# One group of products per attention step on TensorE, in place of two or three, in a two-layer transformer kernel

## The reference

```
# block 1: "dilated" attention, 8 heads of 64, three (window, dilation) patterns
s = q k^T + bias;  s = where(mask, s, NEG);  p = exp(s - max)
o = (p v) / sum(p)          # the three patterns joined by a softmax of their log-sums
# block 2: stick-breaking attention, 8 heads of 64, queries in blocks of 128
z = q k^T * scale;  sp = where(causal, softplus(z), 0)
rest = reverse_cumsum(sp) - sp
w = where(causal, exp(log_sigmoid(z) - rest), 0);  o = w v
```

## Time and profile before

| | us |
|---|---|
| three timed runs | 1364.08, 1364.75, 1364.88 |
| their median | 1364.75 |
| profiled execution, first to last instruction (span) | 1363.0 |
| TensorE busy in it | 1355.1 |
| VectorE, ScalarE, POOL busy | 872.2, 817.7, 335.4 |
| first attention on TensorE, from, to | 171.3, 231.5 |
| second attention on TensorE, from, to | 673.2, 793.4 |

### The profile page before, as it was taken

How to read it: one execution, slowest core, us unless ns; L and a number is a source line. 1 busy time by engine, 2 the same in 40 slices (tenths; PEclk the granted TensorE clock), 3 DMA queues, 4 the chain that set the end, 5 groups by cost and what they waited for, 6 DMA issues and landing times.

```text
span 1363.0 us, 19642 instructions
## 1 busy us (share of the span) xinstructions
PE 1355.1 (99%) x7510; PEld 1136.7 (83%) x7510; DVE 872.2 (64%) x1604; ACT 817.7 (60%) x1267; POOL 335.4 (25%) x306
## 2 busy tenths in 40 slices
PE   9999999999999999999999999999999999999999
PEld 6977966789899898887777878888888898889889
DVE  6055466577576672356498789975436785558557
ACT  6575666753544545666488677775656645754553
POOL 0211100235353251111211111211113262315214
DMA  7976643925436138876765575668888536824723
GB/s 250 241 170 137 148 117 86 224 32 195 99 101 175 34 124 192 192 169 143 154 138 122 132 198 124 134 145 184 196 212 206 113 137 174 185 47 160 191 52 109
DMA packets 57970, 202.46 MB, mean 149 GB/s; under 512 B 6450, under 2 KB 7019, under 8 KB 57748
## 3 DMA queue, kind: packets, MB, share of 16 engines
q0 software_dynamic: 25632, 93.09, 36.7%
q1 hardware_dynamic: 31380, 106.24, 23.6%
q10 hardware_dynamic: 864, 1.87, 0.4%
HBM read 199.05 MB, written 2.12 MB: 148 GB/s over the span
## 4 chain that ended last, share of the span: by engine, by line
PE 93%; ACT 2%; DMA 2%; DVE 1%; POOL 1%; issue 1%; SPq 0%; ACTq 0%; POOLq 0%; DVEq 0%
PE bank L644 23%; PE bank L651 23%; PE bank L648 23%; PE bank L682 15%; PE bank L840 2%; PE bank L816 2%; PE bank L830 1%; PE bank L797 1%; PE bank L865 1%; DMA WH<-in_w_in 1%; DMA RAW<-in_w_in 1%; PE bank L848 1%; POOL quarters_s L2182 0%; DMA quarters<-in_w_ff 0%; POOL quarters L2182 0%
## 5 line engine op out<-in xcount | busy, mean ns | idle before, releaser
L644 PE MATMUL bank<-NH,WH 128*128 128x512 f32 x1152 | 463.3, 403 | 0.4 <-ACT NH L1191 0.2
L648 PE MATMUL bank<-NL,WH 128*128 128x512 f32 x1152 | 448.2, 390 | 0.5 <-DVE NL L1453 0.5
L651 PE MATMUL bank<-NH,WL 128*128 128x512 f32 x1152 | 448.1, 390 | 0.4 <-DVE WL L1448 0.4
L644 PEld LDWEIGHTS bank<-NH,WH 128*128 128x128 f32 x1152 | 216.5, 188 | 62.1 <-issue 19.7
L651 PEld LDWEIGHTS bank<-NH,WL 128*128 128x128 f32 x1152 | 216.2, 188 | 46.7 <-DVE WL L1448 0.8
L648 PEld LDWEIGHTS bank<-NL,WH 128*128 128x128 f32 x1152 | 216.5, 188 | 45.4 <-issue 2.6
L1010 ACT ACTIVATE WH<-RAW 128x1024 fp32r<-128x1024 f32 (+3 forms) x148 | 151.9, 1031 | 76.4 <-PE bank L651 39.5
L682 PE MATMUL bank<-AH,WH 128*128 128x256 f32 x644 | 182.6, 284 | 0.5 <-DVE gains_hT L1830 0.3
L682 PE MATMUL bank<-AL,WH 128*128 128x256 f32 x644 | 182.2, 283 | 0.0
L682 PE MATMUL bank<-AH,WL 128*128 128x256 f32 x644 | 182.2, 283 | 0.0
L1018 ACT ACTIVATE WL<-WH 128x1024 fp32r<-128x1024 f32 (+1 forms) x146 | 153.2, 1051 | 21.4 <-DMA WH<-in_w_in 19.1
(11 more groups left out here) (371 smaller groups left out, 2130.5 us busy)
## 6 DMA issues: line engine op xcount, KB each, us to landing
WL<-in_w_in POOLq DMA_DIRECT2D x58, 512.0 KB, 6.3
RAW<-in_w_gu SPq DMA_DIRECT2D x44, 512.0 KB, 5.4
WL<-in_w_gu POOLq DMA_DIRECT2D x34, 512.0 KB, 7.8
RAW<-in_w_ff SPq DMA_DIRECT2D x32, 512.0 KB, 4.7
WH<-in_w_in POOLq DMA_DIRECT2D x32, 512.0 KB, 6.4
RAW<-in_w_in SPq DMA_DIRECT2D x28, 512.0 KB, 6.3
quarters<-in_w_ff SPq DMA_DIRECT2D x24, 512.0 KB, 4.7
WL<-in_w_ff POOLq DMA_DIRECT2D x17, 512.0 KB, 6.1
```

Source lines behind the costliest of these rows:

```text
L644: e.matmul(o, a[0], a[1], start=(k == 0), stop=False)
L648: e.matmul(o, b[0], b[1], start=False, stop=False)
L651: mm = e.matmul(o, c[0], c[1], start=False, stop=(k == t.kt - 1))
```

## The change

The generator `attention` gets a function `when(s)` in place of a start, a step and an offset. All three kinds of product of a step are due at one time, in the order transposes, scores, values. In the first attention that is the step's start (the scores move forward by 0.57 units); in the second it is 3.36 units after the start, where the scores stood, and 1.68, 0 and -3.36 in the last three steps, which have no scores. On ScalarE the exponential of the second attention now stands before the copies to wT, and on VectorE the copy out (`heads_out`) is due after the group. The mask or bias step of the first attention is due with the scores, 0.57 units earlier.

```diff
+        def dil_time(s):
+            return T_A1 + R1 * s
+
+        def stick_time(s):
+            return T_A2 + R2 * s + 1.68 * (2 if s < NA else (1, 0, -2)[s - NA])
...
-            def attention(name, T, R, q, apart, qs, ks, vs, zbuf, wbuf, q_key, k_key, v_keys, fence):
+            def attention(name, when, qs, ks, vs, zbuf, wbuf, q_key, k_key, v_keys, fence):
                 for s in range(NA + 3):
-                    yield T + R * s + 0.1
+                    yield when(s) + 0.1
                     if s == 0:
                         pe.wait_ge(*fence)
+                    if 2 <= s <= NA + 1:
+                        hp, i = ORDER[s - 2]
+                        for p in range(2):
...
+                                mm = e.transpose(bank[:, j * P:(j + 1) * P], z[:, j * P:(j + 1) * P], ident)
+                            mm.then_inc(*pe.sig(name + "_t", s - 2, p))
+                    if s < NA:
...
+                            e.matmul(FB[p][:, 0:n], qs[64 * p:64 * p + 64, hp, i * P:(i + 1) * P],
+                                     ks[64 * p:64 * p + 64, hp, 0:n], start=True, stop=True).then_inc(*pe.sig(name + "_z", s, p))
                     if s >= 3:
                         hp, i = ORDER[s - 3]
...
-                        if apart:
-                            yield T + R * s + q
-                    if 2 <= s <= NA + 1:
...
-                    if s < NA:
-                        yield T + R * s + (2 * q if apart else q)
...
                     if s < NA and ORDER[s][1] < NT - 1:
-                        yield T_A1 + R1 * s + 2 * 0.57 + 0.02
+                        yield T_A1 + R1 * s + 0.57 + 0.02
                         exponentials(s)
...
+                    if 2 <= s <= NA + 1:
+                        yield stick_time(s) + 0.6
...
+                            e.activation(wT[p][:, 0:n], FB[2 + p][:, 0:n], ACT.Copy).then_inc(*act.sig("stick_w", s - 2, p))
...
                     if s < NA:
-                        yield T_A1 + R1 * s + 2 * 0.57
+                        yield T_A1 + R1 * s + 0.57
...
-                    if s >= 3:
-                        yield T_A2 + R2 * s + 0.2
+                    if s > NA:
+                        yield stick_time(s) + 0.6
                         heads_out("stick", s - 3, lambda hp: mixed2[:, hp, :], [])
...
+                    if 3 <= s <= NA:
+                        yield stick_time(s) + 0.6
+                        heads_out("stick", s - 3, lambda hp: mixed2[:, hp, :], [])
```

More of the change, by code:

```diff
@@ L799, in sum_values @@
                 mm.then_inc(*pe.sig(name, h))
-            def attention(name, T, R, q, apart, qs, ks, vs, zbuf, wbuf, q_key, k_key, v_keys, fence):
+            def attention(name, when, qs, ks, vs, zbuf, wbuf, q_key, k_key, v_keys, fence):
                 for s in range(NA + 3):
-                    yield T + R * s + 0.1
+                    yield when(s) + 0.1
                     if s == 0:
                         pe.wait_ge(*fence)
+                    if 2 <= s <= NA + 1:
+                        hp, i = ORDER[s - 2]
+                        for p in range(2):
+                            bank, z = FB[2 + p], zbuf[2 * ((s - 2) % 2) + p]
+                            pe.wait_ge((name + "_p", s - 2, p))
+                            if s >= 3:
+                                pe.wait_ge((name + "_w", s - 3, p))
+                            for j in range(i + 1):
+                                mm = e.transpose(bank[:, j * P:(j + 1) * P], z[:, j * P:(j + 1) * P], ident)
+                            mm.then_inc(*pe.sig(name + "_t", s - 2, p))
+                    if s < NA:
+                        hp, i = ORDER[s]
+                        n = (i + 1) * P
+                        for p in range(2):
+                            pe.wait_ge(q_key(hp), k_key(hp))
+                            if s:
+                                pe.wait_ge((name + "_b", s - 1, p))
+                            e.matmul(FB[p][:, 0:n], qs[64 * p:64 * p + 64, hp, i * P:(i + 1) * P],
+                                     ks[64 * p:64 * p + 64, hp, 0:n], start=True, stop=True).then_inc(*pe.sig(name + "_z", s, p))
                     if s >= 3:
@@ L1156, in stick @@
                 for s in range(NA + 3):
[L1157 to L1166, removed]
                     if 1 <= s <= NA:
@@ L1174, in stick @@
                             e.activation(z, z, ACT.Exp).then_inc(*act.sig("stick_p", s - 1, p))
+                    if 2 <= s <= NA + 1:
+                        yield stick_time(s) + 0.6
+                        hp, i = ORDER[s - 2]
+                        n = (i + 1) * P
+                        for p in range(2):
+                            act.wait_ge(("stick_t", s - 2, p))
+                            if s >= 3:
+                                act.wait_ge(("stick_o", s - 3, p))
+                            e.activation(wT[p][:, 0:n], FB[2 + p][:, 0:n], ACT.Copy).then_inc(*act.sig("stick_w", s - 2, p))
                     if s < NA:
```

5 lines of the change are left out of this document (2 added, 3 removed).

## The result

| | before | after |
|---|---|---|
| median of six runs each (us) | 1364.82 | 1374.88 |
| lowest, highest | 1363.40, 1367.98 | 1373.64, 1377.67 |
| profiled execution: span | 1363.0 | 1374.6 |
| its granted clock, mean | 1.000 | 0.998 |

The ratio is 1.0075, with an interval of 1.0064 to 1.0085: 10.1 us slower, where 5.7 was forecast. 1374.88 lies at the very end of the range (1374.9). The profiled execution of after took 1375.98 us, with 1374.6 from first to last instruction.

The account below looks back on a forecast made before the run. TensorE's own stream plus its waits was taken as the bound. Changes of shape -4.6, first attention's waits +7.2 and second's +3.1 gave +5.7 us: 1364.75 to 1370.5 us, range 1366.3 to 1374.9.

Parts of the forecast that it names:

- changes of shape, both attentions: TensorE, both attentions: each step goes from four changes of array shape to three; -4.6 us, bounds -8.2 and +0.9.
- T of block 3, first attention: Transposes of block 3 wait 1.5 us in each of four head pairs, behind ScalarE's copy and exponentials and VectorE's scaling; +6.0 us.
- groups after the copy out: First attention, after values of block 3: in two head pairs the next transposes wait 0.55 us behind VectorE's output copy; +1.1 us.
- small waits: Other steps of the first attention: 0.5 us at one scores group, 0.3 and 0.2 at the first steps; +2.2 us.
- waits of before that go: First attention: the waits TensorE has there now, seven late starts, are taken off; -2.1 us.
- waits, second attention: Second attention: transposes of block 3 wait 1.2 us in the second head pair, the last transposes 1.9; +3.1 us, bounds 0 and +4.
- clock at half level, both: TensorE's clock in both attentions: the prediction has no term for it, counted as 0.
- tail: The stretch behind the second attention: the prediction has no term for it, counted as 0.
- rival 2: Going from scores to values pays both changes of shape: 5.5 us more, some 1 us of it into waits; 1375 us, chance 0.12.
- Rival 1: Changes of shape go and the waits stay covered: -4.6 us, 1360.2 us, chance 0.06.
- rival 3: Only block 3's chain in the first attention counts, the 1.1 and 3.1 us hidden but for 0.7: +2.2, 1367.0 us, chance 0.16.
- rival 4: Joining groups saves nothing and the waits of now only change places: 1364.75 us, chance 0.04.

Follow-up runs that it names:

- Run 3: Change in the first attention only, second as before, with four pT buffers in place of two; 1367.21 us, 1.0008 of the kernel before.
- run 5: First attention only in one group per step, order values, transposes, scores; second attention as before; 1364.87 us, 1.0005 of the kernel before.
- Run 10: Changed kernel with one edit: in the first attention VectorE's copy out stands behind its reciprocal and scaling; 1372.71 us, 1.0055 of the kernel before.
- run 4: First attention only in one group per step, order transposes, values, scores; second attention as before; 1367.99 us, 1.0022 of the kernel before.
- run 6: Change in the second attention only, with ScalarE's copies to wT ahead of the exponentials; first as before; 1365.25 us, 1.0000 of the kernel before.
- run 2: Change in the second attention only, first attention as before; 1366.85 us, 1.0013 of the kernel before.
- run 8: Changed kernel with four pT buffers and, in the first attention, VectorE's copy out behind its scaling; 1365.69 us, 1.0006 of the kernel before.
- run 9: Change in the second attention only, copies to wT ahead of exponentials, last three groups due at 1.68 units each; 1365.67 us, 1.0002 of the kernel before.
- run 11: Changed kernel with four pT, copy out behind scaling, copies to wT first, last three groups at 1.68 units; 1364.56 us, 0.9995 of the kernel before.
- run 1: Change in the first attention only, second attention as before; 1373.44 us, 1.0057 of the kernel before.

## Why the prediction was right in sign and short in size

The direction, the long waits and who waits for whom came out as forecast; the sum was 4.4 us short. Two steps failed: the walk through the groups behind VectorE's copy out, which stopped at T, and the clock, which was put at nothing without a reason. By its terms, measured from the starts in the profiled executions:

| us | forecast | measured |
|---|---|---|
| changes of shape, both attentions | -4.6 | -4.5 |
| T of block 3, first attention | 6.0 | 6.5 |
| groups after the copy out | 1.1 | 3.15 |
| small waits | 2.2 | 2.35 |
| waits of before that go | -2.1 | -2.2 |
| waits, second attention | 3.1 | 3.9 |
| clock at half level, both | 0 | 3.1 |
| tail | 0 | -2.15 |
| sum | 5.7 | 10.15 |

- **Changes of shape: right.** The join that no row showed (S to V) was taken as 0.14 late at V's first pass and is seen as 0.20 saved per step. The work of the groups without waits fell by 1.8 and 2.7 us. The Trainium skill (TensorEngine Tiling, Tiling Modes) says that changing the mode drains TensorE; by the trace going from S to V, rows to columns, costs one change and not two, which refutes rival 2, though the time came out where it had put it: that is chance.
- **T of block 3: right**, 1.6 us four times for a forecast of 1.5. Run 3 shows the cause by its buffer, run 5 by the order.
- **"Where one triple stands there (two head pairs of four), the next T waits 0.55: 1.1 us. Where two stand, nothing": this step failed.** The wait of T was right (0.6, twice). The walk stopped at T. The group has S right behind, whose second head needs VectorE's mask, and that stands behind the same copy out: 0.6 to 0.7 more at each of three groups, that with two triples included, so that the term is 3.15 us and not 1.1. In the order of before these scores started 3.8 us after the values of block 3 had ended, now 2.15. Run 10 separates the two halves, 0.7 and 0.56.
- **The clock: put at nothing, the largest miss: this step failed too.** Waits of 1.6 to 2.3 us were counted at their own length. Behind one of the four in the first attention and behind the last in the second TensorE ran at half level for 3.4 us, and lost 1.5 us each time. Runs 3, 4, 5, 6 and 10 take waits away, and none has a fall in the attention that they mend, though run 10 keeps the four of 1.6 us. A fall comes in some executions and not in others: of the six timed ones of after, the profiled one has a mean clock of 0.998, as two falls make it, the other five 0.999.
- **Second attention: right in cause** (run 6), 1.7 and 2.3 for 1.2 and 1.9. At the first of the two TensorE came 12.3 us after S and not 12.9: the walk took off the changes of shape and T, but not that values of three blocks had left this stretch and those of one block had come in, 0.4 us. At the last, VectorE's subtraction ended 1.3 us later after S than before, where 0.5 was assumed.
- **Tail: missed.** "Its own stream plus its waits" was applied to the attentions alone. One wait of 1.6 us stood 16 us behind the second, and took up 1.8 us of the delay in the profiled executions of after and of run 2, but only 0.2 and 0.6 in those of runs 8 and 10. It hangs on when a block of weights lands. In the repaired versions the same wait grows (2.06 us in run 9, 2.17 in run 11) and hides part of their gain. Without what the tail gave back the loss would have been 12.3 us, outside the range: that the time came to lie inside is luck.
- Rival 1 is refuted by the waits, rival 3 by the second attention (3.9 us of waits) and the groups behind the copy out, rival 4 by the 4.5 us that the groups did save.

What stays open: why the clock falls behind one wait of 2 us and not behind another, in the same kernel and even at the same place; that the waits bring it is argued, not shown. No run was made for the fall alone. Its cost of 1.5 us is from single profiled executions; in the timed ones of run 2 those with 0.999 took 1.5 us longer in the mean than those with 1.000 (five and six), in run 9 2.0. Open is also why the load ahead of the recurrence took 5.5 and 5.2 us in the profiles of after and run 2, and 9.1 to 10.3 in all others.

## What to carry to other kernels

Joining groups on the engine that bounds saved changes of shape worth 4.5 us, and lost more than three times that, since the projections between the groups were the cover of three short chains on other engines. Before a group is joined, follow every operand of every member, the last one too and the second head too, to where its producer stands in its queue, and for waits like these (1.6 us and more on TensorE) allow for the clock in the range: here a fall added 1.5 us when it came. And look for the next wait behind the stage: it takes back a delay, and a gain just as well, and if it hangs on a load it does so differently from one execution to the next.

## What the runs showed of the hardware

- Shortly after some waits of 1.6 to 2.3 us (in after, runs 1, 2, 8, 10 and 11), TensorE was granted 0.50 of its clock for 3.4 us, though it was busy by then. After others just as long it was not (three of four in the first attention of after, 2.06 us in run 9). At the low level values passes took 0.42 us in place of 0.27, and 128x512 projections started 0.43 apart in place of 0.23.
- Two heads' scores on 64 rows each run beside each other: four passes of 512 columns take 1.13 us. If the second head starts 0.48 us late, as at 212.0 us in after, the group takes 0.47 us longer (1.60): it pays the whole delay.
- Going from products on 64 rows of the array straight to products on 64 columns costs about as much as one change from whole to part, not two: a group of transposes, scores and values takes 2.06 us, apart they take 2.26.
- The load of one weight block, at the same place in the program, took 5.2 us from issue to landing in run 2 and 9.8 in run 8, which have the same code around it.
